# First attention of a decoder trunk: where eight transposes stand, and what the first four scores wait for

## The reference

```python
lat = xn @ w_in
c_q, c_kv = rmsnorm(lat[..., :384], g_q), rmsnorm(lat[..., 384:640], g_kv)
k_rope = rope(lat[..., 640:], positions)
q = (c_q @ w_uq).reshape(B, S, 8, 128 + 64)       # q_nope, q_rope = rope(...)
kv = (c_kv @ w_ukv).reshape(B, S, 8, 128 + 128)   # k_nope, v
s = (einsum('bqhd,bkhd->bhqk', qn, k_nope) + einsum('bqhr,bkr->bhqk', qr, k_rope)) * scale
p = softmax(where(k_idx <= q_idx, s, NEG_INF))
o = einsum('bhqk,bkhd->bqhd', p, v)
h = h + o @ w_o
```

## Time and profile before

| | us |
|---|---|
| median of 3 runs | 1349.49 (1349.39 to 1351.43) |
| the profiled execution | 1351.96 |
| its span | 1350.2 |
| first attention, from first score to output product | 69.4 to 105.8 |

### The profile page before, as it was taken

How to read it: one execution, slowest core, us unless ns; L and a number is a source line. 1 busy time by engine, 2 the same in 40 slices (tenths; PEclk the granted TensorE clock), 3 DMA queues, 4 the chain that set the end, 5 groups by cost and what they waited for, 6 DMA issues and landing times.

```text
span 1350.2 us, 20418 instructions
## 1 busy us (share of the span) xinstructions
PE 1249.1 (93%) x8367; PEld 639.6 (47%) x8368; DVE 319.0 (24%) x707; ACT 251.3 (19%) x445; POOL 27.9 (2%) x44
## 2 busy tenths in 40 slices
PE   6999999999899699999969998999987999889996
PEld 4754777778665533433423433333342343333342
DVE  2254576766353310010001010010001101001001
ACT  2232433333153011010101101102110111100211
POOL 2100000000200000000000000000000000000000
PEclk9969999999999799999989999999998999999998
DMA  9510745337521469999969999999997999999970
GB/s 340 184 62 0 264 173 187 125 125 250 196 110 55 180 277 419 420 418 418 419 266 419 419 419 421 420 419 418 419 418 314 421 418 420 419 420 418 418 314 33
DMA packets 82370, 413.74 MB, mean 306 GB/s; under 512 B 7622, under 2 KB 12860, under 8 KB 82028
## 3 DMA queue, kind: packets, MB, share of 16 engines
q1 hardware_dynamic: 80908, 409.59, 75.5%
q0 software_dynamic: 1088, 1.81, 0.4%
q10 hardware_dynamic: 288, 1.05, 0.2%
HBM read 411.38 MB, written 1.05 MB: 305 GB/s over the span
## 4 chain that ended last, share of the span: by engine, by line
PE 75%; DMA 7%; SPq 7%; DVE 4%; issue 4%; ACT 2%; POOL 0%; DVEq 0%; ACTq 0%; POOLq 0%
PE ps L1354 11%; PE ps L1334 10%; SPq L627 6%; PE ps L1420 6%; PE ps L1329 5%; PE ps L1312 5%; PE ps L1073 4%; PE ps L1069 4%; PE ps L1070 4%; DMA ring<-in_moe_w_down 4%; DMA ring<-in_moe_w_up 3%; PE ps L1316 3%; PE ps L1384 2%; PE ps L1404 2%; PE ps L1305 2%
## 5 line engine op out<-in xcount | busy, mean ns | idle before, releaser
L1354 PE MATMUL ps<-ring,arena 128*64 128x448 f32 x640 | 256.4, 552 | 40.9 <-issue 25.7
L1355 PE MATMUL ps<-ring,arena 128*64 128x448 f32 x640 | 256.9, 554 | 0.0
L1354 PEld LDWEIGHTS ps<-ring,arena 128*64 128x64 f32 x640 | 85.4, 139 | 190.1 <-issue 177.5
L1334 PE MATMUL ps<-ring,arena 128*32 128x448 f32 x1152 | 162.4, 542 | 0.0
L1335 PE MATMUL ps<-ring,arena 128*32 128x448 f32 x384 | 161.0, 542 | 0.0
L1420 PE MATMUL ps<-ring,arena 128*64 128x512 f32 x280 | 126.3, 597 | 3.4 <-DMA ring<-in_moe_w_down 3.3
L1863 DVE TENSOR_TENSOR arena<-arena,ps 64x448 f32<-64x448 f32 (+1 forms) x64 | 38.5, 613 | 384.4 <-ACT arena L862 205.6
L1421 PE MATMUL ps<-ring,arena 128*64 128x512 f32 x280 | 126.3, 597 | 0.0
L1329 PE MATMUL ps<-ring,arena 128*32 128x448 f32 x768 | 91.2, 546 | 9.6 <-DMA ring<-in_moe_w_up 5.6
L1334 PEld LDWEIGHTS ps<-ring,arena 128*32 128x32 f32 x1152 | 48.1, 111 | 94.5 <-issue 94.5
L1635 DVE TENSOR_TENSOR w_lo<-ring,w_hi 128x2048 fp32r<-128x2048 f32 x33 | 75.5, 2292 | 60.2 <-ACT w_hi L760 58.7
(11 more groups left out here) (278 smaller groups left out, 1484.2 us busy)
## 6 DMA issues: line engine op xcount, KB each, us to landing
ring<-in_moe_w_down SPq DMA_DIRECT2D x128, 896.0 KB, 18.3
ring<-in_moe_w_gate SPq DMA_DIRECT2D x127, 896.0 KB, 21.5
ring<-in_moe_w_up SPq DMA_DIRECT2D x127, 896.0 KB, 22.8
ring<-in_ffn_w_gate SPq DMA_DIRECT2D x5, 2048.0 KB, 7.7
ring<-in_ffn_w_up SPq DMA_DIRECT2D x5, 2048.0 KB, 7.7
ring<-in_ffn_w_down SPq DMA_DIRECT2D x5, 2048.0 KB, 7.8
ring<-in_mla_w_o SPq DMA_DIRECT2D x2, 2048.0 KB, 23.9
ring<-in_swa_w_q SPq DMA_DIRECT2D x2, 2048.0 KB, 8.3
```

What stands on the lines that cost most here:

```text
L1334: pe.matmul(ps[32 * j:32 * j + 32, c, 0:CH], thirds[j], wu[:, c * CH:(c + 1) * CH], start=first, stop=last)
L1354: pe.matmul(ps[0:NARROW, c, 0:CH], lhs, wu[:, cols], start=(k == 0), stop=(k == KD - 1))
L1355: mm = pe.matmul(ps[64:64 + NARROW, c, 0:CH], lhs, wg[:, cols], start=(k == 0), stop=(k == KD - 1))
```

## The change

On TensorE the eight transposes of `qr`, with their wait for `qrope_ready`, move from behind the value products to ahead of them, and ahead of the wait for `krT_ready`. The one wait for all four value copies ahead of the scores (`v_ready` 4) is taken out. In its place each of the scores 0 to 3 waits for the copy of its own bank (`v_ready` i + 1). The waits for `qk_ready` and `qrT_ready` stay where they were. No other engine's program is touched.

```diff
                 mm.then_inc(s.qk_mm, 1)
+            pe.wait_ge(s.qrope_ready, 4)
+            for k in range(4):
+                for t in range(TT):
+                    mm = pe.transpose(ps[:, 4 + k // 2, (k % 2) * S + t * P:(k % 2) * S + (t + 1) * P],
+                                      qr[:, t, k * P:(k + 1) * P], ident)
+            mm.then_inc(s.qrT_mm, 1)
             pe.wait_ge(s.krT_ready, 1)
             for n in range(4):
                 t, half = n // 2, n % 2
...
                 mm.then_inc(s.ukv_v_mm, 1)
-            pe.wait_ge(s.qrope_ready, 4)
-            for k in range(4):
-                for t in range(TT):
-                    mm = pe.transpose(ps[:, 4 + k // 2, (k % 2) * S + t * P:(k % 2) * S + (t + 1) * P],
-                                      qr[:, t, k * P:(k + 1) * P], ident)
-            mm.then_inc(s.qrT_mm, 1)
 
             def scores(i):
                 b, part = i % 4, 64 * (i % 2)
                 if i >= 4:
                     pe.wait_ge(s.s_ready, i - 3)
+                else:
+                    pe.wait_ge(s.v_ready, i + 1)
...
             pe.wait_ge(s.qk_ready, 8)
-            pe.wait_ge(s.v_ready, 4)
             pe.wait_ge(s.qrT_ready, 4)
```

## The result

| | before | after |
|---|---|---|
| median | 1350.37 us (5 runs, 1349.39 to 1354.08) | 1341.14 us (5 runs, 1336.80 to 1342.42) |
| ratio | | 0.9923, 95% interval 0.9897 to 0.9949 |
| profiled execution, its span | 1351.96, 1350.2 | 1340.87, 1339.1 |

The account below looks back on a forecast made before the run. TensorE at half clock was taken to bound the first attention. Gains of 1.67 idle, 0.62 on score 0, 5.06 on scores 1 to 3, 1.88 and 1.59 on steps 0 and 1 made 10.8: 1349.49 to 1338.7 us, range 1336 to 1346.5.

Parts of the forecast that it names:

- The idle time: TensorE between value products and first score: the first score starts at 67.75 instead of 69.42, 1.67 us gained.
- The handover: TensorE's passage from value products to the first score: may need some tenths, 0 to 0.3 us in the range.
- The clock: First attention on TensorE: granted clock held at 1.00 without the idle time, 10.8 us gained in all, chance 0.70.
- "No help for the clock" (C): First attention: the clock falls as soon as before, only 1.67 us gained, 1347.8 us; chance 0.08.
- "a second fall" (B): First attention: the scores alone let the clock down later; 4.0 us gained if after two scores, 1345.5 us; chance 0.17.
- step 0: First step of the head loop behind scores 0 to 3, without value products: 2.40 us at full clock.
- steps 1 to 3: Full head-loop steps, each three transposes, three product pairs and one score: 3.04 us each at full clock.
- rival D: Head loop: clock falls after two scores and stays low until the output products; 3.4 us slower, 1352.9; chance 0.05.
- The pairing: TensorE's clock falls where idle time is followed by products of 64 rows with gaps; the change removes the idle half.
- the own range: Whole-kernel median if the clock holds: 1336 to 1341.5 us, allowing for score size, handover and later short half-clock stays.

Follow-up runs that it names:

- the long idle time: The changed kernel with VectorE copying the transposes twice more behind the last value product and the scores waiting for it: 1355.13 us, ratio 1.0031.

## Why the prediction held, and by how much it missed

- **The idle time.** Forecast 1.67 us, first score at 67.75; measured 67.72. The handover cost nothing. The moved transposes, copies and load cost nothing, each with the cover that was named: the transposes started at 59.97 with the rotation done, the last value copy ended at 68.5 while score 3 started at 73.88.
- **The clock.** Forecast 0.70 for a clock at 1.00 through the attention; it was, in both traces. That the idle time was the cause is shown by filling it (the gain comes without the move) and by putting it back (the gain goes). "No help for the clock" (C) and "a second fall" (B) have no case in any trace. The rule of the Trainium skill behind B ("TensorE: Matmul & The Clock Gate", "A second HAM failure mode: psum-queue depth-cycling") isn't borne out by scores in four banks, not at double length either. The skill tells of small idle times between the groups, though, and these traces show TensorE busy for 100% of the scores, so they don't test the rule's own case.
- **The sizes.** A score at full clock was forecast at 2.06 and took 2.09; step 0 2.40 against 2.37; steps 1 to 3 3.04 each, as forecast; the end of the last score 87.51 against 87.46. A half-clock step was put at 5.55 in rival D, and 5.56 was measured with the long idle time. There the rise came a step later than before, in step 2, which is a part of what that rival told, and it took 1.3 us more idle time as well.
- **The pairing.** The prediction said that the clock fell where idle time was followed by products of 64 rows with gaps. As a condition for the fall that doesn't hold: the 2.83 us of idle time in the dense mixer let the clock down ahead of full-height products in 11 of 14 traces, and the trace of before, the one read, is one of the three without. What the products behind it bear on is how long the low clock lasts: about 3.4 us there, 20.3 in the scores. Whether the low rows matter, or the exposed weight loads, isn't told by any run. The prediction also looked at two falls alone, when a mean clock of 0.97 over 1350 us is some 80 us at half clock.
- **The step that was mis-sized** is the last one, from the profiled execution to the median. The profiled executions differ by 11.1 us, against 10.8 forecast (1340.87 against 1341.2); the 10.88 at the end of the attention is what the forecast was about, while it is luck that the 1.3 us lost in the dense mixer and the 1.5 won at the end nearly cancel. But the prediction took the median of after to be 2.5 us below its profiled execution, as before, and 1338.7 became 1341.14: after, it was 0.3 above. The median gain is 9.2 us, and 1341.14 is close to the upper end of the own range, 1341.5. And it took the fall as certain in every execution before, when 18 of 108 didn't have it. A median hides that share. The new stay at half clock in the dense mixer, 1.3 us, is of the size that the own range allowed for.

## What to carry to other kernels

A short idle time on TensorE can cost many times its length: 1.67 us cost 9 more here, in five executions of six by their times. What stands behind it sets the price. Behind 2.83 us of idle time dense products had the clock back after about 3.4 us; the scores stayed at half clock for 20.3. Look in the clock line for dips and at what stands ahead of them, then move full-height work into the gap; here even useless products did. Where one profile shows a fall or none, look at the spread of the runs before you price it, since the same program does both. Products of different height in turn cost about 0.2 us at each change here (0.39 us for the two that a score was spared), so put those of one height next to each other.

## What the runs showed of the hardware that was not expected

- The same 1.6 us of idle time ahead of the same scores let the clock down in most executions and not in others. Runs in the upper group: none of 17 without idle time, 2 of 12 above 1345.9 with 0.72 us, 8 of 12 with 1.55 (the profiled one of these, 1346.31, had the clock at 1.00, so the group isn't an exact count of falls), 8 of 12 with 1.62 (the split wait alone), 90 of 108 with 1.67, 12 of 12 with 3.01.
- At half clock 20.3 us of mostly scores at 100% busy didn't raise it, and at full clock 16.8 us of scores didn't lower it, in two traces: over these lengths this work kept the clock that it found.
- The same 2.83 us of idle time ahead of dense products let the clock down in 11 of 14 traces, and each time for about 3.4 us.
- A change in the attention gave 3.0 and 4.6 us of unexplained waiting on TensorE among the closing products, 1240 us later, in the two traces of the scores made twice.
